# Adding the experts' rows to their tokens in memory instead of storing each pick and joining them at the end

## The chip, the cores and the metric
One NeuronCore of a Trainium2 chip runs the whole layer as one program. Five engines run instruction streams of their own and meet by semaphores: TensorE (PE), VectorE (DVE), ScalarE (ACT), GpSimd (POOL) and SyncE (SP). SP and POOL issue the transfers; sixteen DMA engines carry them. The metric is the device time of one execution in microseconds.

## The reference
A hybrid encoder layer over 768 tokens of width 1024 (512 "sample" tokens and 256 "prompt" tokens, each group with its own modulation vectors), all in f32: normalise, project, neighbourhood attention beside bidirectional RWKV-7, project, add; then a mixture of experts, add, and a final RMS norm. What matters here is the mixture and what follows it:

```
h   = rms_norm(x) * (1 + scale2) + shift2
pg  = softmax(h @ rg_w + rg_b)            # 4 groups, top 1
le  = (h @ re_w + re_b)[chosen group]     # 8 experts, top 2, weights renormalised
out[token] += w * ((silu(h @ w1[e]) * (h @ w3[e])) @ w2[e])      # two picks e per token, 32 experts
x   = x + gate2 * out
y   = rms_norm(x) * final_g
```

Expert weights are 32 x (w1, w3: 1024 x 512; w2: 512 x 1024), 201 MB in all.

## The kernel before
Tokens stand in six tiles of 128 (four of the sample group, two of the prompt group). The program has numbered phases; the change begins in phase 5.

**Phase 5, residual and routing.** For tile t = 1 to 5 (tile 0 is done earlier) TensorE multiplies by the output weights, VectorE adds the gated result to the input rows in `x2(t)` (`residual`, semaphore `x2_ready`, two halves a tile), normalises them to `h2` (`norm`, `h2_ready`), and SP stores `h2` to memory (`h2_rows`). TensorE transposes the rows (`turned`) and multiplies them by the router's weights (`routed`); VectorE makes the logits (`scores`). After the last tile VectorE alone selects the group and the two experts for all six tiles at once (`first_max`, three times, and masks `both_e`), TensorE counts ranks inside each expert by triangular products, VectorE turns a rank into a slot, and TensorE makes tables by one-hot products: `idx_all`, for every expert and each of its 64 slots the token to gather, and `put_all`, for the 128 half rows of its output the place to write. Experts with more than 64 tokens get further blocks from an overflow list in memory. `list_ready` is given at the end of VectorE's routing, when the list and the two weights of each token, `wts`, are there. Unused slots get an index outside the table and are skipped by the transfer.

**SP's queue in phase 5** is an order written by hand. Weights are kept in three slots of w1, w3 and w2. Slot 0 and w2 of slot 1 are loaded early. After `o5_mm` reaches 12 (the last product with the output weights) follow w1 of slot 1, the last tile's h2 store, w3 of slot 1 and w1 of slot 2, then w3 of slot 2, and behind `list_ready` the overflow lists and w2 of slot 2, the ninth load.

**Phase 6, experts.** Per expert e: GpSimd gathers 64 rows of h2 by an indirect DMA (`xg`, L2346); TensorE transposes them (L2442), multiplies by w1 and w3 (L2455, 64 products each 256 wide), ScalarE applies silu, VectorE multiplies (L2421), TensorE transposes (L2464), multiplies by w2 (L2473); VectorE copies the output from PSUM to `yb` (L2425: partition p < 64 is the first half of the row of slot p, partition 64 + p its second half); GpSimd scatters the 128 half rows of 2 KB to `y_dram`, which has a row for each of the two picks of each token (L2335). GpSimd's order is gather e, wait for the landing of scatter e - 4 (`freed`), scatter e - 3. As soon as TensorE has used a weight slot, SP loads the weights of expert e + 3 into it (L2309). The overflow blocks would follow in a loop at run time; in this data there are none. When TensorE has done all but the last two experts SP also loads the rows of gate2 (`g2_row`) and of final_g (`f_row`).

**Phase 7, join and final norm.** SP waits for `picks_out` and loads for each tile both picks (1 MB). For tile 0 ScalarE and VectorE weight and add them; for tiles 1 to 5 TensorE adds them by products with diagonal matrices of the weights (L2577), VectorE multiplies by the gate (L2546) and adds x2 (L2548). ScalarE squares with a running sum (L2528) and takes the root (L2529), VectorE takes the reciprocal (L2558) and scales (L2560), SP stores the tile (L2511).

Of the kernel before, what the change touches and what calls it, by code (L numbers as in the profile page):

```python
# [21 lines left out]
f16 = mybir.dt.float16  # L22
# [130 lines left out]
def build(nc, A, O, upto=4):  # L153
    ctx = ExitStack()
    with ctx:
# [32 lines left out]
        y_dram = dram("pick_out", [2 * TOK * 2, D // 2])  # L188
# [1663 lines left out]
        g2_row = take(2 * D).rearrange("p (g d) -> p g d", g=2)  # L1852
# [25 lines left out]
        idx_all = take(NBLK).bitcast(i32)  # L1878
# [5 lines left out]
        put_all = take(NBLK).bitcast(i32)  # L1884
# [43 lines left out]
        tmp_e = arena[:, top6:top6 + N2 * NE].rearrange("p (n e) -> p n e", e=NE)  # L1928
        wrap = take(NBLK)
        lsel = take(NT * NE).rearrange("p (t e) -> p t e", e=NE)  # L1930
        hits16 = take(NT * NE // 2).bitcast(f16).rearrange("p (t e) -> p t e", e=NE)
        rank12, first12, excl12, pos12, low12, base12 = (take(N2) for _ in range(6))
        level = take(N2 * (TOK // BLK - 1)).rearrange("p (n m) -> p n m", n=N2)
        rank16 = take(N2 * BLK // 2).bitcast(f16).rearrange("p (n s) -> p n s", n=N2)
        block16 = take(N2 * NBLK // 2).bitcast(f16).rearrange("p (n b) -> p n b", n=N2)
# [4 lines left out]
        o32 = take(NE)  # L1940
        assert top[0] <= at_prep, top[0]

        WEIGHTS = (("h1_mm", w1_f, w1_v), ("h3_mm", w3_f, w3_v), ("y_mm6", w2_f, w2_v))

        def sp_phase5(sp):
# [38 lines left out]
            sp.dma_start(slot_dram.rearrange("(b s) o -> b (s o)", s=BLK), over_idx[NE:NBLK]).then_inc(sem("list_out"), 16)  # L1984
            sp.dma_start(put_dram.rearrange("(b s) o -> b (s o)", s=2 * BLK), over_put[NE:NBLK]).then_inc(sem("list_out"), 16)
# [7 lines left out]
        def act_phase5(act, own):  # L1993
            for t in range(1, NT):
                if t == 3:
                    rec_out(act, NT - 2)
                    rec_out(act, NT - 1)
                h2T_evac(act, t - 1, 0)
                h2T_evac(act, t - 1, 1)
                tile_square(act, own, t, 0)  # L2000
                if t == NT - 1:
                    h2T_evac(act, t, 0)
                tile_square(act, own, t, 1)
            h2T_evac(act, NT - 1, 1)
            act.wait_ge(sem("g_centred"), 1)
            nc.scalar.activation(tg, tg, ACT.Exp).then_inc(sem("g_exp"), 1)
            act.wait_ge(sem("m_diff"), 1)
            nc.scalar.activation(m2, m2, ACT.Exp).then_inc(sem("m_exp"), 1)
# [44 lines left out]
        def dve_phase5(dve, own):  # L2053
# [9 lines left out]

            for t in range(1, NT):
# [11 lines left out]
            scores(NT - 1)  # L2076

            dve.wait_ge(sem("logit_ready"), NT)

            def b(ap, shape):  # L2080
                return ap.unsqueeze(len(ap.shape)).to_broadcast(shape)

            def first_max(one_hot, top_v, values, tmp, width):

                shape = [P, NT, width]
                own.link(nc.vector.tensor_reduce(top_v, values, AX, ALU.max))
                own.link(nc.vector.tensor_tensor(tmp, values, b(top_v, shape), ALU.is_equal))
                own.link(nc.vector.tensor_tensor(tmp, tmp, fall_row[:, 0:width].unsqueeze(1).to_broadcast(shape), ALU.mult))
                own.link(nc.vector.tensor_reduce(pk, tmp, AX, ALU.max))
                own.link(nc.vector.tensor_tensor(one_hot, tmp, b(pk, shape), ALU.is_equal))  # L2090

            pg = logit[:, :, 0:NG]
            first_max(og, gm, pg, tg, NG)

            le = logit[:, :, NG:].rearrange("p t (g e) -> p t g e", g=NG)
            own.link(nc.vector.tensor_tensor(lsel.rearrange("p t (g e) -> p t g e", g=NG), le, b(og, [P, NT, NG, EPG]), ALU.mult))
            own.link(nc.vector.tensor_reduce(s8, lsel.rearrange("p t (g e) -> p t e g", g=NG), AX, ALU.add))
            first_max(o1, m1, s8, t8, EPG)
            own.link(nc.vector.scalar_tensor_tensor(s8, o1, -1e30, s8, ALU.mult, ALU.add))
            first_max(o2, m2, s8, t8, EPG)  # L2100
            for one, o8 in ((both_e[:, 0], o1), (both_e[:, 1], o2)):
                own.link(nc.vector.tensor_tensor(one.rearrange("p t (g e) -> p t g e", g=NG), b(og, [P, NT, NG, EPG]),
                                                 o8.unsqueeze(2).to_broadcast([P, NT, NG, EPG]), ALU.mult))
            nc.vector.tensor_tensor(hits16, both_e[:, 0], both_e[:, 1], ALU.add).then_inc(sem("hits_ready"), 1)

            picks = both_e.rearrange("p k t e -> p (k t) e")
            pairs = [P, N2, NE]

            def picked(out, values):

                own.link(nc.vector.tensor_tensor(tmp_e.rearrange("p (k t) e -> p k t e", k=2), both_e, values, ALU.mult))
                own.link(nc.vector.tensor_reduce(out, tmp_e, AX, ALU.add))

            picked(first12, first_row.unsqueeze(1).unsqueeze(1).to_broadcast([P, 2, NT, NE]))
            dve.wait_ge(sem("rank_mm"), 2)
            own.link(nc.vector.tensor_copy(cnt_col[0:NE], bank[3][0:NE, 0:1]))
# [3 lines left out]
            picked(rank12, bank[2][:, 0:NT * NE].rearrange("p (t e) -> p t e", e=NE).unsqueeze(1).to_broadcast([P, 2, NT, NE]))  # L2120
            own.link(nc.vector.tensor_tensor(level, rank12.unsqueeze(2).to_broadcast([P, N2, TOK // BLK - 1]),
                                             first_row[:, 1:TOK // BLK].unsqueeze(1).to_broadcast([P, N2, TOK // BLK - 1]), ALU.is_ge))
            own.link(nc.vector.tensor_reduce(low12, level, AX, ALU.add))
            own.link(nc.vector.scalar_tensor_tensor(low12, low12, -float(BLK), rank12, ALU.mult, ALU.add))
            own.link(nc.vector.tensor_tensor(rank16, low12.unsqueeze(2).to_broadcast([P, N2, BLK]),
                                             rank_row.unsqueeze(1).to_broadcast([P, N2, BLK]), ALU.is_equal))
            nc.vector.tensor_tensor(rank16, rank16, token_row.unsqueeze(2).to_broadcast([P, N2, BLK]), ALU.mult).then_inc(sem("rank16_ready"), 1)
# [3 lines left out]
            picked(excl12, excl.unsqueeze(1).unsqueeze(1).to_broadcast([P, 2, NT, NE]))  # L2131
            own.link(nc.vector.tensor_scalar(base12, excl12, float(NE - 1), float(BLK), ALU.add, ALU.mult))
            own.link(nc.vector.tensor_tensor(base12, base12, first12, ALU.subtract))
            own.link(nc.vector.scalar_tensor_tensor(base12, rank12, float(BLK), base12, ALU.is_ge, ALU.mult))
            own.link(nc.vector.tensor_tensor(pos12, rank12, first12, ALU.add))
            own.link(nc.vector.tensor_tensor(pos12, pos12, base12, ALU.add))
            own.link(nc.vector.tensor_tensor(base12, pos12, low12, ALU.subtract))
            nc.vector.tensor_tensor(block16, base12.unsqueeze(2).to_broadcast([P, N2, NBLK]),
                                    block_row.unsqueeze(1).to_broadcast([P, N2, NBLK]), ALU.is_equal).then_inc(sem("block16_ready"), 1)
            dve.wait_ge(sem("idx_mm"), 1)  # L2140
            own.link(nc.vector.tensor_scalar(wrap[0:BLK], bank[5][0:BLK, 0:NBLK], float(-TOK), float(-TOK), ALU.is_ge, ALU.mult))
            nc.vector.scalar_tensor_tensor(idx_all[0:BLK], bank[5][0:BLK, 0:NBLK], float(2 * TOK), wrap[0:BLK], ALU.add, ALU.add).then_inc(sem("idx_ready"), 1)
            dve.wait_ge(sem("idx_mm"), 2)
            nc.vector.tensor_scalar(put_all, bank[2][:, 0:NBLK], 2.0, half_place, ALU.mult, ALU.add).then_inc(sem("put_ready"), 1)
# [7 lines left out]
            dve.wait_ge(sem("idx_mm"), 3)  # L2152
            own.link(nc.vector.tensor_scalar(tmp_e.rearrange("p n e -> p (n e)")[0:NBLK, 0:BLK], bank[3][0:NBLK, 0:BLK], float(-TOK), float(-TOK), ALU.is_ge, ALU.mult))
            nc.vector.scalar_tensor_tensor(over_idx[0:NBLK], bank[3][0:NBLK, 0:BLK], float(2 * TOK), tmp_e.rearrange("p n e -> p (n e)")[0:NBLK, 0:BLK], ALU.add, ALU.add)
            for j in range(2):
                nc.vector.tensor_scalar(over_put[0:NBLK, j * BLK:(j + 1) * BLK], bank[3][0:NBLK, 0:BLK], 2.0, float(4 * TOK + j), ALU.mult, ALU.add)
# [510 lines left out]
```

## Time and profile before

| | |
|---|---|
| median of three runs | 1367.01 us (1366.73 to 1368.69) |
| the profiled execution's own time | 1364.02 us |
| its span, first to last instruction | 1362.3 us |
| TensorE busy | 1162.7 us, 85% |
| VectorE busy | 416.6 us, 31% |
| ScalarE busy | 347.9 us, 26% |
| GpSimd busy | 280.0 us, 21% |
| moved by DMA | 314.74 MB, 231 GB/s over the span |
| granted TensorE clock, mean | 0.955 |

The page is one execution seen by the hardware profiler. Busy shares are means over stages that have different limits, so a stage is read by its windows and its waits. A line of the timeline has its start in microseconds from the span's beginning, its length, engine, source line and operation; in brackets stands how long the engine was idle before and who released it. An engine letter with q (SPq, POOLq) is that engine's queue at the moment of issue; the transfer itself then takes until its landing. The share of DMA can pass 1 by a few hundredths.

### The profile page before, as it was taken

Reading aid. Unit: us, or ns where it says so; the run is one execution under the profiler, and the core shown is the slowest. Engines: PE = TensorE matmul, PEld = TensorE weight load, DVE = VectorE, ACT = ScalarE, POOL = GpSimd, SP = SyncE. Lnnn points to the kernel's source line nnn. Section 1 sums busy time; section 2 is a strip of 40 time slices with the busy share of each in tenths; the row PEclk is TensorE's granted clock in tenths of the full one; section 3 lists DMA queues with packets and bytes.
Section 4 is the critical chain, followed back from the end, with each engine's and each line's share of the span. In section 5 each row is a group of like instructions: output and inputs, shape, how many; then the busy total and the mean of one; then the engine's idle time right before and its main releaser. Section 6 shows DMA issues by size and latency. Waiting matters only on the chain.

```text
span 1362.3 us, 29631 instructions
## 1 busy us (share of the span) xinstructions
PE 1162.7 (85%) x13063; PEld 721.1 (53%) x13063; DVE 416.6 (31%) x726; ACT 347.9 (26%) x749; POOL 280.0 (21%) x254
## 2 busy tenths in 40 slices
PE   4899999999996889988799939998877778778855
PEld 3465555564455778878655525554444444444432
DVE  2100044435655555665446360000000000000017
ACT  3210024443332555566422111010010010100002
POOL 0100002312245434367331001111111111111000
PEclk8999999999997999999999969998899998998897
DMA  9895141223254221230408079999999999999975
GB/s 316 290 338 207 31 139 63 78 85 107 95 172 114 50 50 28 50 81 4 179 32 324 31 283 381 390 394 405 401 396 406 400 404 404 396 396 402 414 284 223
DMA packets 82025, 314.74 MB, mean 231 GB/s; under 512 B 13808, under 2 KB 28488, under 8 KB 65150
## 3 DMA queue, kind: packets, MB, share of 16 engines
q1 hardware_dynamic: 75862, 298.96, 59.2%
q0 software_dynamic: 5120, 12.59, 2.6%
q8 instruction: 87, 1.43, 0.4%
q10 hardware_dynamic: 936, 1.61, 0.3%
q14 instruction: 20, 0.16, 0.0%
HBM read 291.58 MB, written 25.74 MB: 233 GB/s over the span
## 4 chain that ended last, share of the span: by engine, by line
PE 28%; DMA 27%; DVE 5%; ACT 4%; issue 2%; SPq 1%; POOL 0%; DVEq 0%; POOLq 0%; ACTq 0%
DMA arena<-in_exp_w 26%; PE bank L1568 10%; PE bank L2455 6%; PE bank L1838 6%; PE bank L2473 2%; PE bank L1592 2%; SPq L2309 1%; DVE arena L1449 1%; PE bank L2194 1%; DMA arena<-pick_out 1%; PE bank L2442 1%; DVE arena L1436 1%; ACT arena L1278 1%; DVE arena L2560 0%; PE bank L2577 0%
## 5 line engine op out<-in xcount | busy, mean ns | idle before, releaser
L2455 PE MATMUL bank<-arena 128*64 128x256 f32 x2048 | 253.6, 405 | 72.6 <-DMA arena<-in_exp_w 59.8
L888 PE MATMUL bank<-arena 128*128 128x512 f32 (+1 forms) x736 | 256.2, 496 | 4.1 <-DVE arena L488 2.0
L2455 PEld LDWEIGHTS bank<-arena 128*64 128x64 f32 x2048 | 157.9, 146 | 178.3 <-DMA arena<-in_exp_w 69.5
L1568 PE MATMUL bank<-arena 64*64 64x64 f16 (+3 forms) x7184 | 199.2, 217 | 37.0 <-issue 13.2
L1568 PEld LDWEIGHTS bank<-arena 64*64 64x64 f32 (+2 forms) x7184 | 177.3, 124 | 64.1 <-issue 36.5
L888 PEld LDWEIGHTS bank<-arena 128*128 128x128 f32 x736 | 133.8, 189 | 100.3 <-issue 86.1
L2473 PE MATMUL bank<-arena 128*64 128x512 f32 x512 | 116.9, 598 | 16.6 <-ACT arena L2399 16.6
L2421 DVE TENSOR_TENSOR arena<-bank,arena 128x256 f32<-128x256 f32 x32 | 13.6, 425 | 305.6 <-PE bank L2455 305.6
L2346 POOL DMA_INDIRECT arena<-h_scratch,arena x32 | 30.7, 960 | 363.3 <-PE bank L2442 267.2
L1838 PE MATMUL bank<-arena 128*128 128x512 f32 x192 | 86.4, 597 | 0.0
L2473 PEld LDWEIGHTS bank<-arena 128*64 128x64 f32 x512 | 34.0, 136 | 77.4 <-issue 54.7
L2425 DVE COPY arena<-bank 128x512 f32<-128x512 f32 x32 | 22.1, 692 | 164.4 <-PE bank L2473 164.4
L2386 ACT COPY arena<-bank 128x512 f32<-128x512 f32 x32 | 18.8, 586 | 202.6 <-PE bank L2442 202.6
L2335 POOL DMA_INDIRECT pick_out<-arena x32 | 32.4, 1011 | 172.8 <-DVE arena L2425 172.8
L2393 ACT ACTIVATE arena<-bank 128x256 f32<-128x256 f32 x32 | 12.3, 384 | 209.9 <-PE bank L2455 209.9
L448 POOL TENSOR_TENSOR arena<-arena 128x512 f32<-128x512 f32 x16 | 18.6, 1163 | 191.0 <-DVE arena L761 191.0
L1838 PEld LDWEIGHTS bank<-arena 128*128 128x128 f32 x192 | 34.9, 189 | 37.9 <-issue 37.3
L1462 DVE CAST arena<-bank 128x512 f16<-128x512 f32 x48 | 32.9, 686 | 38.9 <-PE bank L1568 38.9
L923 PE MATMUL bank<-arena 128*128 128x512 f32 x96 | 42.9, 598 | 0.0
L2442 PEld LDWEIGHTS bank<-arena 64*128 64x128 f32 x256 | 30.6, 199 | 16.3 <-issue 16.3
L722 DVE COPY arena<-bank 128x512 f32<-128x512 f32 (+1 forms) x8 | 4.5, 559 | 113.8 <-PE bank L888 113.7
L2442 PE MATMUL bank<-arena 64*128 64x64 f32 x256 | 35.0, 278 | 4.3 <-DMA arena<-h_scratch,arena 4.3
(262 smaller groups left out, 1276.5 us busy)
## 6 DMA issues: line engine op xcount, KB each, us to landing
arena<-in_exp_w SPq DMA_DIRECT2D x96, 2048.0 KB, 44.8
arena<-in_ada_w SPq DMA_DIRECT2D x12, 2048.0 KB
arena<-in_w_in SPq DMA_DIRECT2D x11, 1024.0 KB, 6.6
direction_scratch<-arena SPq DMA_DIRECT2D x6, 1536.0 KB, 6.1
arena<-direction_scratch SPq DMA_DIRECT2D x24, 384.0 KB, 5.6
arena<-pick_out SPq DMA_DIRECT2D x6, 1024.0 KB, 10.3
arena<-in_x_sample SPq DMA_DIRECT2D x8, 512.0 KB, 5.0
arena<-in_w_out SPq DMA_DIRECT2D x8, 512.0 KB, 7.1
```

What stands on the lines that cost most here:

```text
L888: return nc.tensor.matmul(bank[i % 3][:, 0:GR[p] * GW], w[:, k, :], hT[:, k, PART[p]], start=(k == 0), stop=(k == KD - 1))
L923: ins = nc.tensor.matmul(bank[i % 3], hT[:, k, c * P:(c + 1) * P], wv[:, k, :], start=(k == 0), stop=(k == KD - 1))
L1462: nc.vector.tensor_copy(nm[1 + l % 2][:, 1], bank[6].rearrange("p (j r c) -> p j r c", j=NPAIR, r=2)).then_inc(sem("nm_dve"), 1)
L1568: return nc.tensor.matmul(out, lhsT, r, start=start, stop=True, skip_group_check=True)
L1592: ins = nc.tensor.transpose(bank[q % 2][:, j * P:(j + 1) * P], src[:, j * P:(j + 1) * P], ident)
L1838: ins = nc.tensor.matmul(out_bank(t, hf), catT[:, k, t * P:(t + 1) * P], wout[k][:, hf * 512:hf * 512 + 512], start=(k == 0), stop=(k == K ...
L2335: nc.gpsimd.indirect_dma_start(y_dram, bass.IndirectOffsetOnAxis(ap=put_all.bitcast(u32)[:, e:e + 1], axis=0), yb[e % 2], None, bounds_che ...
L2346: nc.gpsimd.indirect_dma_start(xg[e % 2][0:BLK, :], None, h2_dram, bass.IndirectOffsetOnAxis(ap=idx_all.bitcast(u32)[0:BLK, e:e + 1], axis=0),
L2425: nc.vector.tensor_copy(yb[c.s], bank[6 + c.s]).then_inc(c.sem("y_ready6"), 1)
L2442: ins = nc.tensor.transpose(bank[0][:, j * BLK:(j + 1) * BLK], xg[c.s][0:BLK, j::KD], ident[0:BLK, 0:BLK])
L2455: ins = nc.tensor.matmul(bank[b + 2 * c.s][BLK * n:BLK * n + BLK, 0:HALF], xT[c.s][:, j, :], slot[c.w][:, j, n * HALF:(n + 1) * HALF], sta ...
L2473: ins = nc.tensor.matmul(bank[6 + c.s][BLK * n:BLK * n + BLK, :], hidT[:, j % 2, j // 2, :], w2_s[c.w][:, j, n * 512:(n + 1) * 512], start ...
```

## The change
Each expert's output is weighted while it is evicted from PSUM, and the scatter adds it to a table of token sums in memory.

- `y_dram` becomes `token_sum`, two half rows per token plus 256 spare half rows. In phase 5 SP stores `x2(t)`, the residual, there before it stores h2.
- The scatter has `compute_op=ALU.add`. Half rows of unused slots are no longer skipped but go to the spare half rows.
- Per expert two VectorE instructions make `gw`, the gate row of each slot's group times the slot's weight (for both groups; one of the two weights is zero), and the eviction is a product with `gw` instead of a copy. The gate rows (`g2_half`, four loads of 64 partitions x 2 KB) come in phase 5 and not near the end of phase 6. VectorE's loop over the experts is written out for all 32.
- A table of the slots' weights, `w_slot`, is made in phase 5 by 24 f32 products, and one for the overflow blocks by 12 more. TensorE waits for `w_slot_ready` before the experts. Two more small stores write the overflow's weights; they stand behind `list_ready`.
- Routing is split: `select` and `ranked` run for tiles 0 to 3 while tiles 4 and 5 are worked on and then for tiles 4 and 5. The main table now holds only the 32 main blocks, and its indices and places come from one product; overflow is treated after them.
- Phase 7 loads one tile of sums of 512 KB each and does only the final norm. TensorE has no work in it. `f_row` has a new place.

```diff
-        y_dram = dram("pick_out", [2 * TOK * 2, D // 2])
+        y_dram = dram("token_sum", [2 * TOK + 2 * P, D // 2])
+        wo_dram = dram("slot_weight", [2 * MAX_OVER * BLK, 1])
...
             def h2_rows(t):
+                sp.wait_ge(sem("x2_ready"), 2 * t + 2)
+                sp.dma_start(token_rows(t), x2(t)).then_inc(sem("sum_in"), 16)
                 sp.wait_ge(sem("h2_ready"), t + 1)
...
             weights(1, 2)
+            for g in range(2):
+                for h in range(2):
+                    at = 5 * D + h * (D // 2)
+                    sp.dma_start(g2_half[h * BLK:(h + 1) * BLK, g, :], mod_dram[g, at:at + D // 2].partition_broadcast(BLK)).then_inc(sem("g2_in"), 16)
             sp.wait_ge(sem("list_ready"), 1)
...
+            for g in range(2):
+                sp.dma_start(wo_dram[g * MAX_OVER * BLK:(g + 1) * MAX_OVER * BLK, :].rearrange("(b s) o -> b (s o)", s=BLK), sums_over[:, g, :]).then_inc(sem("list_out"), 16)
             weights(2, 2)
...
+            act.wait_ge(sem("rank16_ready"), 2)
+            nc.scalar.copy(rank32, rank16).then_inc(sem("rank32_ready"), 1)
+            act.wait_ge(sem("w_slot_mm"), 1)
+            nc.scalar.copy(w_slot, bank[6][:, 0:2 * NE].rearrange("p (g e) -> p g e", g=2)).then_inc(sem("w_slot_ready"), 1)
...
             for t in range(1, NT):
                 residual(dve, own, t)
                 scores(t - 1)
+                if t == NT_S:
+                    select(EARLY)
                 if t < NT - 1:
                     norm(dve, own, t)
+                if t == NT_S:
+                    ranked(EARLY, 1)
...
+            select(LATE)
+            own.link(nc.vector.tensor_tensor(m2, m2, m1, ALU.subtract))
+            nc.vector.tensor_tensor(tg, pg, b(gm, [P, NT, NG]), ALU.subtract).then_inc(sem("g_centred"), 1)
+            ranked(LATE, 2)
...
+            table(LATE).then_inc(sem("idx_mm"), 1)
+            pe.wait_ge(sem("rank32_ready"), 1)
+            pe.wait_ge(sem("w_pick_ready"), 1)
+            for g in range(2):
+                some = group_of_pick(g)
+                for i in some:
+                    for j in range(2):
+                        ins = nc.tensor.matmul(bank[6][j * BLK:(j + 1) * BLK, g * NE:(g + 1) * NE], rank32[:, i, :], w_pick[:, i, :],
+                                               start=(i == some[0]), stop=(i == some[-1]))
+            ins.then_inc(sem("w_slot_mm"), 1)
...
-            for g in range(2):
-                sp.dma_start(g2_row[:, g, :], mod_dram[g, 5 * D:6 * D].partition_broadcast(P)).then_inc(sem("g2_in"), 16)
...
                 if e == 0:
                     pool.wait_ge(sem("put_ready"), 1)
+                    pool.wait_ge(sem("sum_in"), 16 * NT)
...
-                                             bounds_check=4 * TOK - 1, oob_is_err=False).then_inc(sem(f"y_out{e % 2}"), 16)
+                                             bounds_check=2 * TOK + 2 * P - 1, oob_is_err=True, compute_op=ALU.add).then_inc(sem(f"y_out{e % 2}"), 16)
...
+                nc.vector.tensor_scalar(gw, g2_half[:, 1, :], share[1], None, ALU.mult).then_inc(c.sem("gw_done"), 1)
+                dve.wait_ge(c.sem("gw_done"), 2 * c.n + 1)
+                nc.vector.scalar_tensor_tensor(gw, g2_half[:, 0, :], share[0], gw, ALU.mult, ALU.add).then_inc(c.sem("gw_done"), 1)
...
-                nc.vector.tensor_copy(yb[c.s], bank[6 + c.s]).then_inc(c.sem("y_ready6"), 1)
+                dve.wait_ge(c.sem("gw_done"), 2 * c.n + 2)
+                nc.vector.tensor_tensor(yb[c.s], bank[6 + c.s], gw, ALU.mult).then_inc(c.sem("y_ready6"), 1)
+                dve.wait_ge(c.sem("y_ready6"), k)
...
+            pe.wait_ge(sem("w_slot_ready"), 1)
             rows(Main(0, 0, 0, 0, 0, 0))
...
             for t in range(NT):
-                sp.dma_start(ya[t], picks[t]).then_inc(sem(f"rows_in{t}"), 16)
+                sp.dma_start(x2(t), token_rows(t)).then_inc(back_in(t)[0], 16)
...
             for t in range(NT):
-                act.wait_ge(sem("joined"), t + 1)
+                act.wait_ge(*back_in(t))
```

The routing functions that are new (`select` has 21 instructions, those of before on the tiles `ts`):

```python
            def select(ts):
                n = ts.stop - ts.start
                dve.wait_ge(sem("logit_ready"), ts.stop)
                first_max(og, gm, pg, tg, NG, ts)
...
                nc.vector.tensor_tensor(hits16[:, ts], both_e[:, 0, ts], both_e[:, 1, ts], ALU.add).then_inc(sem("hits_ready"), 1)

            def table(ts):
                turn = 1 if ts is EARLY else 2
                pe.wait_ge(sem("rank16_ready"), turn)
                pe.wait_ge(sem("picks16_ready"), turn)
                for k in range(2):
                    for t in range(ts.start, ts.stop):
                        i = k * NT + t
                        for j in range(2):
                            ins = nc.tensor.matmul(bank[0][j * BLK:(j + 1) * BLK, 0:NE], rank16[:, i, :], picks16[:, i, :],
                                                   start=(i == 0), stop=(i == 2 * NT - 1))
                return ins
```

## Rows read from the trace of the kernel before

**Rows 1.** The page, 40 slices: busy share of the DMA engines in tenths.
```profile
DMA  9895141223254221230408079999999999999975
```

**Rows 2.** Windows: length, busy PE, PEld, DVE, ACT, POOL, clock, DMA share, GB/s.
```profile
1000.00:1200.00 200.00, 154.55 (x1086) 86.14 (x1088) 13.39 (x24) 17.68 (x39) 24.56 (x25) 0.97 1.01 402
...
1275.00:1291.00 16.00, 12.36 (x68) 6.47 (x68) 0.90 (x2) 1.24 (x3) 0.00 (x0) 0.79 1.01 425
```

**Rows 3.** Waits of 920 to 1300 us: engine, line, awaited, total us, times, longest.
```profile
PE bank L2455 <- DMA arena<-in_exp_w: 58.6, 25, 3.4
```

**Rows 4.** Timeline of SP's queue, 700 to 900 us: start, length, what, how many.
```profile
786.78 0.33 SPq L1948 DMA_DIRECT2D arena<-in_exp_w  x1
...
812.61 0.32 SPq L1983 DMA_DIRECT2D overflow_list<-arena  x1
...
813.98 0.41 SPq L1948 DMA_DIRECT2D arena<-in_exp_w  x1
```

**Rows 5.** The chain that ended last, 1270 us to the end: start, length, what.
```profile
1264.94 43.55 DMA arena<-in_exp_w
...
1319.10 2.54 DMA pick_out<-arena
```

**Rows 6.** DMA issues from 600 us: size and median us from issue to landing.
```profile
arena<-in_x_sample SPq DMA_DIRECT2D x4, 512.0 KB, 4.4
```

**Rows 7.** Timeline of the last stage, ScalarE and VectorE.
```profile
1333.55 1.28 ACT L2529 ACT_TABLE_LOAD   x1
...
1353.79 1.06 ACT L2528 ACTIVATE arena<-arena 128x1024 f32<-128x1024 f32 x1 [2.38 <-DVE arena L2548]
...
1354.76 0.19 ACT L2528 ACTIVATION_READ_ACCUMULATOR arena<-arena 128x1 f32 x1
...
1354.97 0.29 ACT L2529 ACTIVATE arena<-arena 128x1 f32<-128x1 f32 x1
...
1355.30 0.16 DVE L2558 RECIPROCAL arena<-arena 128x1 f32<-128x1 f32 x1
...
1355.50 1.28 DVE arena L2560
```

**Rows 8.** DMA queues in 1000 to 1200 us: packets, MB, share of 16 engines.
```profile
q1 hardware_dynamic: 6773, 76.17, 95.0%
...
q0 software_dynamic: 1920, 4.24, 6.0%
```

**Rows 9.** Windows of 2 us around the scatter issued at 971.68 us.
```profile
970.00:972.00 2.00, 2.00 (x22) 1.35 (x20) 0.69 (x1) 0.00 (x0) 0.32 (x1) 1.00 1.04 342
...
972.00:974.00 2.00, 1.60 (x16) 0.78 (x12) 0.00 (x0) 0.36 (x1) 0.69 (x1) 1.00 0.97 289
```

**Rows 10.** Windows of 20 us before the stream.
```profile
740.00:760.00 20.00, 20.00 (x69) 10.52 (x68) 6.02 (x9) 3.65 (x10) 0.00 (x0) 1.00 0.33 120
...
760.00:780.00 20.00, 20.00 (x71) 10.62 (x70) 7.08 (x10) 5.09 (x13) 0.00 (x0) 1.00 0.07 27
```

**Rows 11.** Windows around the ninth weight load.
```profile
810.00:815.00 5.00, 1.11 (x8) 0.95 (x8) 1.86 (x12) 1.02 (x3) 1.09 (x2) 0.50 0.37 96
...
817.00:818.00 1.00, 1.00 (x8) 0.62 (x6) 0.00 (x0) 0.00 (x0) 0.00 (x0) 0.50 0.96 295
```

**Rows 12.** Timeline of VectorE in the routing: first, second, and the indices.
```profile
791.26 0.18 DVE L2086 TENSOR_REDUCE arena<-arena 128x6 f32<-128x24 f32 x1
...
791.47 0.18 DVE L2087 TENSOR_TENSOR arena<-arena 128x24 f32<-128x24 f32 x1
...
807.72 0.21 DVE L2142 SCALAR_TENSOR_TENSOR arena<-bank,arena 64x56 int32<-64x56 f32 x1
```

**Rows 13.** Timeline of TensorE: the first expert's transposes.
```profile
813.26 1.11 PE L2442 MATMUL bank<-arena 64*128 64x64 f32 x8 [4.28 <-DMA arena<-h_scratch,arena]
```

**Rows 14.** The page's groups: busy us, mean ns, idle before, releaser.
```profile
L2421 DVE TENSOR_TENSOR arena<-bank,arena 128x256 f32<-128x256 f32 x32 | 13.6, 425 | 305.6 <-PE bank L2455 305.6
```

**Rows 15.** The tile of the scatters' target: all its DMAs, issue to landing.
```profile
DMA to landing us min/median/max: 2.5/8.3/15.3
```

More of the change, by code:

```diff
@@ L1883, in build @@
         over_put = take(2 * BLK).bitcast(i32)
[L1884 removed]
+        put_all = take(NE).bitcast(i32)
         put_o = take(1).bitcast(i32)
@@ L1940, in build, with back_in, token_rows, group_of_pick @@
         o32 = take(NE)
+        put_a, put_b = take(NE), take(NE)
         assert top[0] <= at_prep, top[0]
+        EARLY, LATE = slice(0, NT_S), slice(NT_S, NT)
         WEIGHTS = (("h1_mm", w1_f, w1_v), ("h3_mm", w3_f, w3_v), ("y_mm6", w2_f, w2_v))
+        def back_in(t):
+            return (sem(f"x5_in{t}"), 16 * (NT_P if t == NT_S else 1) + 16) if t <= NT_S else (sem("last_back"), 16)
+        def token_rows(t):
+            return y_dram[2 * t * P:2 * (t + 1) * P, :].rearrange("(p h) n -> p (h n)", h=2)
+        def group_of_pick(g):
+            return [k * NT + t for k in range(2) for t in range(NT) if group(t) == g]
         def sp_phase5(sp):
@@ L2100, in dve_phase5 @@
[L2100 to L2116, printed above, removed]
+            select(LATE)
@@ L2173, in turned @@
                 for hf in range(2):
+                    if hf and between:
+                        between()
                     pe.wait_ge(sem("x2_ready"), 2 * j + hf + 1)
@@ L2202, in pe_phase5 @@
                 if t == NT - 1:
+                    ranks(EARLY)
                     turned(t - 1)
@@ L2213, in pe_phase5 @@
                     rec_turned(pe, NT - 2)
-            turned(NT - 1)
+            turned(NT - 1, between=lambda: table(EARLY))
             routed(NT - 1)
-            pe.wait_ge(sem("x2_ready"), 2 * NT)
-            pe.wait_ge(sem("hits_ready"), 1)
-            hits = hits16.rearrange("p t e -> p (t e)")
-            n = NT * NE
-            nc.tensor.matmul(bank[2][:, 0:n], before16, hits, start=True, stop=False)
-            for s in range(1, NT):
-                ins = nc.tensor.matmul(bank[2][:, s * NE:n], ones16, hits[:, 0:n - s * NE], start=False, stop=(s == NT - 1))
@@ L2224, in pe_phase5 @@
-            ins.then_inc(sem("rank_mm"), 1)
-            for t in range(NT):
-                ins = nc.tensor.matmul(bank[3][0:NE, 0:1], hits16[:, t, :], ones16[:, 0:1], start=(t == 0), stop=(t == NT - 1))
-            ins.then_inc(sem("rank_mm"), 1)
+            ranks(LATE)
+            for t in range(NT):
+                ins = nc.tensor.matmul(bank[7][0:NE, 0:1], hits16[:, t, :], ones16[:, 0:1], start=(t == 0), stop=(t == NT - 1))
+            ins.then_inc(sem("rank_mm"), 1)
+            table(LATE).then_inc(sem("idx_mm"), 1)
@@ L2483, in pe_phase6 @@
             overflow(pe, over, overflow_count(pe))
-        top[0] = P + 2
-        ya = [take(2 * D).rearrange("p (k d) -> p k d", k=2) for _ in range(NT)]
         top[0] = ARENA - WEXP
```

287 lines of the change are left out of this document (152 added, 135 removed).

## The prediction

> **What bounds the kernel now.** I read the page's forty slices first: the DMA engines are idle or half used for most of the first half and then stand at nine tenths or more from slice 25 to slice 38 [rows 1]. In 1000 to 1200 us their share is 1.01 at 402 GB/s, while TensorE is busy for only 154.55 of 200 us [rows 2]. Next I read the waits of 920 to 1300 us: TensorE waited 25 times for expert weights [rows 3]. So the expert stage is a stream of 96 loads of 2 MB on SP's queue, nearly all of it behind 786.78 us, when the load after the last projection is issued [rows 4]; what makes that stream longer is added to the end in full, and what TensorE, VectorE or GpSimd do beside it is free as long as it stays inside a period of about 16.5 us. Last I read the chain that ended last: the weights issued at 1264.94 land at 1308.5, the last expert is finished, its scatter lands at 1321.64, and from there the last stage runs alone to 1362.3 [rows 5]. The change touches three things: the opening of the stream (routing), its content (the scatters), and the last stage. I price each.
>
> **The last stage (saves).** Before, 40.7 us lie between the last landing and the end of the span [rows 5]. After, no picks are loaded, no product by the diagonal is made (40 matmuls), and no gate, sum or join is left on VectorE; a tile of sums of 512 KB is loaded where the residual stood, ScalarE squares it, VectorE scales it. Hop from landing to SP's issue 0.4 and the issue 0.4; a 512 KB load lands in 4.4, as the x loads did [rows 6]; ScalarE loads its table once, 1.28, and does six tiles at 1.06 + 0.18 + 0.29 = 1.53 us with gaps [rows 7], so 9.2; the six loads are all in within 8 us and VectorE needs 1.28 + 0.17 per tile, so ScalarE sets the pace. Then the last scale, 1.5, and the last store, 5.5 (from 1356.8 to 1362.3 [rows 7]). Sum 0.8 + 4.4 + 1.3 + 9.2 + 1.5 + 5.5 = 22.7, a saving of 18.0. The last scatter now reads before it writes; it took 2.54 [rows 5] and I give it 1.2 more (0.5 to 3). Net **-17**.
>
> **The scatters (cost).** In 1000 to 1200 us the load queue moved 76.17 MB [rows 8]. Where no scatter or gather is issued the engines move 425 GB/s [rows 2]; those bytes alone would take 179.2 us, so 20.8 us went to the 12.1 experts' pairs of a gather and a scatter (76.17 MB by 6.29 MB an expert), 1.72 us a pair. A gather and a scatter move 1536 picks x 4 KB / 32 = 197 KB each, 0.46 us at 425. The gather I take at that, so a scatter costs 1.26 us, more than twice its bytes. The two slices around one scatter say the same: 342 and 289 GB/s in place of 425 for 2 us each [rows 9], 1.03 us lost and 0.46 of its own, 1.5. After, two things change. Unused slots are no longer skipped but sent to 256 spare half rows: 128 rows of 2 KB and not 96, so 1.7 us. And each row is added: its old content must be read too. Nothing in this trace shows an adding DMA, so I bound it. From below: the added bytes written, 65 KB or 0.15 us, and the read hidden beside the write; less than nothing is excluded, since every byte that moved before still moves. From above: adding doubles the whole scatter, 3.4 us, +2.1. In between, the read is charged like the gather's, 262 KB at 425 GB/s, 0.62 us: 2.3 us in all, **+1.0** a scatter, my value, as the gather is the nearest row of a read from memory by rows. 31 scatters, issued from 832.05 to 1304.54, lie before the last weights land: **+31**; bounds +5 and +65.
>
> The trace shows that plain scatters already cost more than their bytes [rows 8, 9]; it does not show why. The Trainium skill ("Collectives: The Full Stack", section "The bandwidth ceiling: the fold count and why AG ≠ RS ≠ AR") says that an add in the DMA datapath is slow not for the arithmetic but because it needs two source reads, both on one ring, and that reduce-scatter ran at about half the rate of a copy. No trace here shows it; by that rule the scatter would double, which is the upper bound and the second rival.
>
> **The opening of the stream (cost).** The first three loads go out at 717, the engines are a third busy in 740 to 760 and 0.07 in 760 to 780 [rows 10], and four more follow from 786.78. The ninth waits for the overflow list at 812.6 and goes out at 813.98 [rows 4]; the queue had run dry, 0.37 busy in 810 to 815, and full rate is back at about 817.2 [rows 11]. After:
> - Routing of the first four tiles is done ahead, in VectorE's gaps of tile 4 and 5. TensorE has no gap there: five or so products of 0.06 us, +0.3 to 0.4 on all that follows.
> - For the last two tiles the 21 selecting instructions shrink little, since at 24 elements they are already 0.18 long in steps of 0.21 [rows 12]: 4.3 us and not 5.7. Two subtractions, the ranks (0.3), eight ranking instructions (2.3), the table on TensorE and two more (1.3): indices ready at about 800.3, before 807.9 [rows 12]. Gathers go out 7.6 us earlier.
> - But TensorE may not start the experts: it stands behind the weight table, 24 small products at 0.14 each by the eight 64 x 64 ones that took 1.11 at half clock [rows 13], done at 806.6; then the overflow's product, nine VectorE instructions (3.5), and 12 + 12 products (0.6 and 2.4 plus latency): 813.5, before 813.26 [rows 13]. The gain of 7.6 is gone.
> - The list is ready after eight more VectorE instructions, 815.4 (+2.9), and two more small DMAs of 0.45 each stand before the ninth load: issued 817.8, **+4**, and nothing else in the stream makes up for it, as what follows was already back to back. New traffic in front of it, the last residual tile (512 KB) and four gate loads of 128 KB, 1.05 MB or 2.5 us, fills part of the hole and is not added again. Bounds -1 and +7: the hole of 5 us is all that could be won.
>
> **Costed at nothing.** Stores of five residual tiles, 1.3 us each of engine time, lie in the idle stretch 745 to 786 or before weights that are not needed until 815; SP waits on x2_ready first, which always precedes the h2_ready that it waits on anyway. Two VectorE instructions per expert for the gate (about 1.4 us) and the wait for its own write: VectorE idled 305.6 us before the hidden product [rows 14]; they run while TensorE does the next w1, which takes 3.4. If that cover went, 32 x 1.4. Eviction times gate is as long as the copy. GpSimd waits for the residual stores before scatter 0, 40 us after they landed; behind it stand freed and the gathers, not late. The gate rows of 2 x 512 KB loaded at 1290 go, but they stood behind the last weights. The unrolled VectorE loop issues what it did.
>
> **Sum.** The profiled execution took 1364.0 (span 1362.3 and 1.7 around). 1364.0 + 4 + 31 - 17 = 1382. The median of the runs shown, 1367.0, is 3.0 above the profiled one: **1385.0**.
>
> **Rivals.**
> - *The add rides along* (faster). The engines read the old row while they stream the new one, and only the bytes written count: +5 for +31, 1359. It decides from below 0.3 us a scatter. For: read and write are two sides of a DMA, and the share of the software queue is small [rows 8]. Against: the stream already pays 1.26 us for 0.46 us of bytes.
> - *Only the spare rows cost*: +0.4 x 31 = 13, 1367, no change.
> - *Adding doubles the scatter*: +65, 1419. [...]
> - *The landing chain binds.* Scatter e goes out only when e - 1 has landed. Landings took 8.3 at the median, 15.3 at most, in periods of 16.5 [rows 15]; if adding doubled the median, 16.6 + 1.0 of issue, each period grows by about 1 and yb comes free late; beyond that it grows one for one, 1420 and more.
>
> **Chances.** Forecast 0.38 (its own range 1370 to 1400), rides along 0.22, spare rows only 0.10, doubled 0.22, landing chain 0.08. Two executions differ by some 0.2% (about 2.7 us), so faster means under 1364.3: rides along and part of the next, 0.26; same 0.09; slower 0.65. Range 1358 to 1422, from the first rival to just past the doubled one.
>
> **What would show it.** The load queue's bytes in 1000 to 1200 us: 76.17 MB in periods of 16.5 us before; 75 MB or more would be the first rival, 72 my forecast (17.5 us), 68 the doubled one (18.6 us). First expert transposes at 813.5 and the ninth load at 817.8. From the last landing to the end 22 us, not 40.7. If TensorE's waits are no longer for weights but for gathers or for yb, the sum is wrong in kind.

## The result, and the profile after

The change made the kernel slightly slower: 1370.06 us median (1365.70 to 1374.48, 18 runs) against 1367.01 (18 runs of the kernel before beside them), a ratio of 1.0027 with the interval 1.0015 to 1.0039, or +3.7 us. A second series (x6 below) gave 1.0038 (1.0024 to 1.0052), +5.2 us; I use the mean of both, +4.4. The forecast was +18. The direction was right, the size off by 14 us. The profiled execution has a span of 1365.1 us.

Below, a ratio is turned into microseconds by 1367, so +4.4 stands for a mean ratio of 1.0032. Single profiled executions differ by up to 5 us in when the stream begins (783.97 to 788.99 us), so effects are taken from ratios, and traces serve for where they sit and as a check.

The slices of the page after, to be held against [rows 1]: the hole in slice 24 is filled, nothing else stands out.

```profile
DMA  9895141232254222130427199999999999999995
```

Windows (columns as in [rows 2]), of the opening and of the stream. From 805 to 820 us the engines were never short of work, where before they were at 0.37 in 810 to 815 [rows 11]. The stream moves 392 GB/s where it moved 402 [rows 2].

```profile
805.00:810.00 5.00, 3.63 (x39) 3.45 (x40) 2.46 (x11) 0.00 (x0) 0.00 (x0) 0.50 1.01 310
810.00:815.00 5.00, 4.13 (x26) 2.58 (x26) 1.31 (x8) 0.58 (x1) 0.93 (x1) 0.53 1.00 287
815.00:820.00 5.00, 5.00 (x50) 3.18 (x46) 1.24 (x2) 1.67 (x2) 0.00 (x0) 1.00 1.03 325
...
1000.00:1200.00 200.00, 158.66 (x1042) 89.78 (x1040) 26.34 (x45) 15.81 (x36) 32.95 (x23) 0.93 1.02 392
```

The DMA queues in 1000 to 1200 us, which answer to [rows 8]: the load queue moved 2.88 MB less, and the packets of GpSimd's queue took 11.3% of the sixteen engines' time, not 6.0%.

```profile
q1 hardware_dynamic: 6500, 73.29, 90.7%
q0 software_dynamic: 2590, 5.04, 11.3%
```

SP's queue in the opening, which answers to [rows 4]. The first load after the projections is at 784.25 and the ninth at 813.47, 29.2 us later; before it was 27.2.

```profile
784.25 0.33 SPq L1972 DMA_DIRECT2D arena<-in_exp_w  x1
...
788.92 7.24 SPq L1972 DMA_DIRECT2D arena<-in_exp_w  x3
796.20 2.39 SPq L2011 DMA_DIRECT2D arena<-mod_scratch  x4
811.47 0.33 SPq L2013 DMA_DIRECT2D overflow_list<-arena  x1
...
813.47 0.41 SPq L1972 DMA_DIRECT2D arena<-in_exp_w  x1
```

TensorE's timeline between the routing and the first expert: the 24 products of the weight table (which leave 48 records), the overflow's products, the transposes of [rows 13] and the first weights.

```profile
799.76 2.78 PE L2328 MATMUL bank<-arena 128*64 128x32 f32 x48 [3.20 <-DVE arena L2195]
...
806.99 2.75 PE L2339 MATMUL bank<-arena 128*24 128x64 f32 x24
809.67 1.14 PE L2557 MATMUL bank<-arena 64*128 64x64 f32 x8
811.68 3.61 PE L2570 MATMUL bank<-arena 128*64 128x256 f32 x18 [0.87 <-ACT arena L2487]
```

The chain that ended last, as in [rows 5]. It still runs through a weight load. The last scatter takes 4.76 us (2.54 before), lands at 1344.74, and 20.4 us remain to the end of the span; before they were 40.7.

```profile
1328.33 0.04 issue
1328.38 3.70 PE bank L2570 x32
...
1339.98 4.76 DMA token_sum<-arena
...
1345.15 3.28 DMA arena<-token_sum
1348.45 1.15 ACT arena L2629 x2
1349.62 1.28 ACT L2630
...
1359.28 1.28 DVE arena L2638
```

TensorE's waits of 920 to 1300 us, as in [rows 3]: still for weights. GpSimd has a new wait, for the landing of a scatter, ahead of its gather; no wait of TensorE for a gather follows from it.

```profile
PE bank L2570 <- DMA arena<-in_exp_w: 46.1, 27, 3.0
...
POOL arena L2447 <- DMA token_sum<-arena: 60.6, 6, 10.3
```

So three sizes are in question: what a stored scatter costs, what the add costs on top, and what the opening cost. The experiments take these one by one.

### The profile page after: what moved, and what is told of

Same layout as the page of the kernel before. It is cut to its first block, busy times and chain, and to the rows that moved or that the text cites. A ratio compares the mean times of both kernels' runs of the same rounds, so it can differ in the third digit from the quotient of the medians.

```text
span 1365.1 us, 29717 instructions
## 1 busy us (share of the span) xinstructions
PE 1162.9 (85%) x13087; PEld 729.0 (53%) x13087; DVE 444.7 (33%) x800; ACT 347.3 (25%) x750; POOL 309.1 (23%) x254
## 4 chain that ended last, share of the span: by engine, by line
DMA 29%; PE 28%; ACT 5%; DVE 4%; issue 2%; SPq 1%; POOL 0%; DVEq 0%; ACTq 0%; POOLq 0%
DMA arena<-in_exp_w 28%; PE bank L1569 10%; PE bank L2570 6%; PE bank L1839 6%; PE bank L2588 2%; PE bank L1593 2%; SPq L2408 1%; DVE arena L1450 1%; PE bank L2293 1%; PE bank L2557 1%; DVE arena L1437 1%; ACT arena L2629 1%; ACT arena L1279 1%; ACT arena L1269 0%; DVE arena L1467 0%
## 5 line engine op out<-in xcount | busy, mean ns | idle before, releaser
L2570 PE MATMUL bank<-arena 128*64 128x256 f32 x2048 | 262.9, 415 | 76.0 <-DMA arena<-in_exp_w 53.2
L2570 PEld LDWEIGHTS bank<-arena 128*64 128x64 f32 x2048 | 164.2, 149 | 186.6 <-issue 66.9
L2436 POOL DMA_INDIRECT token_sum<-arena x32 | 60.9, 1904 | 181.5 <-DVE arena L2538 167.7
L2533 DVE TENSOR_TENSOR arena<-bank,arena 128x256 f32<-128x256 f32 x32 | 13.6, 424 | 270.6 <-PE bank L2570 270.6
L2588 PEld LDWEIGHTS bank<-arena 128*64 128x64 f32 x512 | 37.6, 138 | 83.7 <-issue 55.1
L2538 DVE TENSOR_TENSOR arena<-bank,arena 128x512 f32<-128x512 f32 x32 | 22.1, 691 | 173.9 <-PE bank L2588 173.9
L2494 ACT ACTIVATE arena<-bank 128x256 f32<-128x256 f32 x32 | 12.3, 383 | 249.4 <-PE bank L2570 249.4
L1314 ACT CAST arena<-bank 128x512 f16<-128x512 f32 x60 | 35.6, 593 | 4.5 <-PE bank L1569 4.4
```

The costliest lines, as they stand in the source:

```text
L1314: nc.scalar.copy(xs[3 if l == XP else 1 + l % 2].rearrange("p g j c -> p (g j c)"), bank[7]).then_inc(sem("x_ready"), 1)
L2436: nc.gpsimd.indirect_dma_start(y_dram, bass.IndirectOffsetOnAxis(ap=put_all.bitcast(u32)[:, e:e + 1], axis=0), yb[e % 2], None, bounds_che ...
L2570: ins = nc.tensor.matmul(bank[b + 2 * c.s][BLK * n:BLK * n + BLK, 0:HALF], xT[c.s][:, j, :], slot[c.w][:, j, n * HALF:(n + 1) * HALF], sta ...
L2588: ins = nc.tensor.matmul(bank[6 + c.s][BLK * n:BLK * n + BLK, :], hidT[:, j % 2, j // 2, :], w2_s[c.w][:, j, n * 512:(n + 1) * 512], start ...
```

## The experiments

Every kernel was timed beside the kernel before: x2, x6, x9 and x10 twelve times, the others, whose output is not the layer's, four to six times. "After" is the changed kernel; a minus sign means faster than before.

**Stored or added, 128 or 96 half rows (x1, x2, x3).** The three differ from the kernel after only in the arguments of the scatter:

```diff
-    bounds_check=2 * TOK + 2 * P - 1, oob_is_err=True, compute_op=ALU.add)
+    bounds_check=2 * TOK + 2 * P - 1, oob_is_err=True)                     # x1: stores, 128
+    bounds_check=2 * TOK - 1, oob_is_err=False, compute_op=ALU.add)        # x2: adds, spare rows skipped
+    bounds_check=2 * TOK - 1, oob_is_err=False)                            # x3: stores, spare rows skipped
```

In x1 and x3 the sums are not formed: a store overwrites what stood there. x2 computes everything.

> The changed kernel with its scatter storing instead of adding; all 128 half rows still go out. It leaves out the summing, so the output is not the layer's. Theory A, a price per half row that the add raises a little (from the traces: 1.26 us for 96 stored, 1.96 us for 128 added, so 13 and 15 ns a half row): 31 x 0.28 = 9 us less than the changed kernel, about 1361. Theory B, the spare half rows are free and the whole +0.70 us per expert is the add: 31 x 0.70 = 22 less, 1348. Theory C, the stream pays the time for which a lone scatter holds the sixteen engines (2.08 us added against 0.51 x 128/96 = 0.68 stored): 43 less, 1327. Last stage as in the changed kernel (20 us) in all three.

> The changed kernel with the index bound set so that half rows of unused slots are skipped, as the kernel before did; the add stays and the result is the same. Theory A: 32/128 of 1.96 us less per scatter, 0.49 x 31 = 15 less than the changed kernel, about 1355, faster than both kernels. Theory B (spare rows free): no change, 1370. Theory C: a quarter of 2.08, 0.52 x 31 = 16 less, 1354; it differs from A in the other runs. A lone last scatter holds the engines for about 1.6 us and not 2.08 by C and by A alike.

> The changed kernel with both undone: the scatter stores and skips unused slots, just the traffic of the kernel before; it leaves out the summing. Theories A and B: 0.70 x 31 = 22 less than the changed kernel, about 1348, and a period of 16.7 us per expert as before. Theory C: 49 less, 1322. If it is much above 1348, something other than the scatters (the gate rows' VectorE work, the opening) lengthens the stream.

| kernel | half rows | mode | ratio (interval) | us against before |
|---|---|---|---|---|
| after, two series | 128 | add | 1.0027 (1.0015 to 1.0039), 1.0038 (1.0024 to 1.0052) | +4.4 |
| x1 | 128 | store | 0.9892 (0.9870 to 0.9915) | -14.8 |
| x2, two series | 96 | add | 0.9971 (0.9959 to 0.9983), 0.9961 (0.9946 to 0.9976) | -4.6 |
| x3 | 96 | store | 0.9874 (0.9857 to 0.9891) | -17.2 |

The add costs 19.2 us (some 3.5 uncertain) on 128 half rows, 0.60 us a scatter over 32, and 12.6 (some 3 uncertain) on 96, 0.39 each. About 2 us of the 19.2 are the last scatter, which stands on the chain (4.76 us for 2.70 in x1); the other 31 cost some 0.55 each. Spare rows cost 2.4 us when stored, within the intervals of nothing, and 9.0 us (0.28 each) when added. Of the theories, C is out: it asked for 43 us between after and x1, and 19.2 were measured. A and B are both right on x3 (22 less, 21.6 measured) and each is wrong on a part: A gave the add 9 us, and B gave the spare rows of x2 nothing. The rate of the stream agrees: x3's load queue moved 76.44 MB in 1000 to 1200 us, no less than before.

```profile
q1 hardware_dynamic: 6786, 76.44, 95.1%
q0 software_dynamic: 1926, 4.24, 5.9%
```

**No rows scattered, then none gathered (x4, x7).** Each is the kernel after with an index bound of 0, so that all but index 0 is skipped by the transfer: in x4 the scatters write next to nothing of the experts' rows, in x7 the gathers also bring next to none, so the experts work on what lies in the buffer.

```diff
-    bounds_check=2 * TOK + 2 * P - 1, oob_is_err=True, compute_op=ALU.add)
+    bounds_check=0, oob_is_err=False, compute_op=ALU.add)                  # x4 and x7
-    bounds_check=TOK - 1, oob_is_err=False)
+    bounds_check=0, oob_is_err=False)                                      # x7, the gather
```

> The changed kernel with an index bound of 0, so that hardly any half row leaves; GpSimd still issues every scatter. It leaves out the experts' part of the sum. Gives the whole price of a scatter in the stream. Theory A: 1.96 x 31 = 61 less than the changed kernel, 1309. Theory B the same total. Theory C: 2.08 x 31 = 64 less, 1306. If the scatter's excess over its bytes came from the gather instead (0.46 + 0.80 both ways swapped), only 1.16 x 31 = 36 less, 1334.

> The changed kernel with neither scatters nor gathers (index bound 0 for both; the experts compute on what stands in their buffers). It leaves out the gather of the rows and the experts' part of the sum. x4_none showed that a stored scatter of 96 half rows costs only 0.43 us and not 1.26, so the excess over the bytes that I charged to scatters must lie elsewhere. Theory D, in the gather: 1.3 us each, so 40 us less than x4_none, about 1295, and over 84 MB of weights in 1000 to 1200 us. Theory E, in neither, 425 GB/s just isn't the rate of a long stream: the gather costs its bytes, 0.46, 14 less, 1321, and 78 to 79 MB.

x4 ran at 0.9776 (0.9759 to 0.9792), -30.6 us; x7 at 0.9430 (0.9408 to 0.9453), -77.9 us. So the 32 stored scatters of x3 cost 13.4 us together (some 3 us uncertain), **0.42 each**, what their 197 KB take at 425 GB/s (0.46), and not the 1.26 of the prediction. The 32 gathers cost 47.3 us (some 4 uncertain), **1.48 each** for as many bytes, three times what I gave them. The pair was priced about right (1.90 measured, 1.72 predicted) and charged to the wrong half. Of the expectations for x4 the swapped one (36 us less than after) met the 35.0 measured, and for x7 theory D (40 less than x4, 47.3 measured) came near. The gathers were switched off only where no rows were scattered; how the two act together is not measured.

A check from the profiled executions, one of each (x5, x6 and x10, which is x2 again, are told below): the time from the first load after the projections to the landing of the last scatter. For x4 and x7 it is read from these lines:

```profile
785.80 0.33 SPq L1972 DMA_DIRECT2D arena<-in_exp_w  x1
...
1308.17 2.69 DMA token_sum<-arena
```

```profile
787.29 0.33 SPq L1972 DMA_DIRECT2D arena<-in_exp_w  x1
...
1262.88 2.69 DMA token_sum<-arena
```

| kernel | first load to last scatter's landing, us |
|---|---|
| before; x5 | 534.9; 535.8 |
| after; x6 | 560.5; 561.2 |
| x1 | 539.7 |
| x2; x10 | 552.8; 549.7 |
| x3 | 536.1 |
| x4 | 525.1 |
| x7 | 478.3 |

By this measure 32 gathers cost 46.8 us, 32 stored scatters 11.0, the add 21.2 on 128 half rows and 15.1 on 96: the same picture within 3 us. The load queue's bytes in 1000 to 1200 us order the kernels in the same way but are too coarse for the smallest price: 76.44 MB in x3 and 77.11 in x4 would be 0.14 us a scatter.

The queues of x4, then of x7, in 1000 to 1200 us:

```profile
q1 hardware_dynamic: 6877, 77.11, 97.0%
q0 software_dynamic: 2768, 2.36, 4.2%
```

```profile
q1 hardware_dynamic: 7555, 84.66, 100.4%
q0 software_dynamic: 3056, 0.02, 0.9%
```

They show where a gather's time goes. Without gathers a megabyte of weights occupies the engines for 200.8 / 84.66 = 2.37 us, with gathers for 194.0 / 77.11 = 2.52. In 77.11 MB that is 11.1 us, 0.91 for each of the 12.3 gathers in the window. The gathers' own packets take 3.3% of 200 us (4.2 less 0.9 for skipped indices), 0.54 each. 0.91 + 0.54 = 1.45: most of a gather's price is that the weights' packets beside it become slower. Why they do is not shown.

And the dips of 2 us that I had read as the scatter's [rows 9] are the gather's. In x4, where no rows are scattered, they stand as deep; in x7 they are gone:

```profile
1000.00:1002.00 2.00, 2.00 (x22) 1.34 (x20) 1.80 (x3) 0.00 (x0) 0.90 (x1) 1.00 1.02 342
1002.00:1004.00 2.00, 1.54 (x16) 0.71 (x10) 0.14 (x1) 0.38 (x1) 0.78 (x1) 1.00 0.97 285
```

```profile
1000.00:1002.00 2.00, 1.84 (x18) 1.26 (x20) 0.00 (x0) 0.00 (x0) 0.00 (x0) 1.00 1.04 422
1002.00:1004.00 2.00, 2.00 (x20) 1.18 (x17) 0.06 (x1) 0.00 (x0) 0.00 (x0) 1.00 1.09 447
```

**The last stage alone (x5).** The kernel before, whose last stage loads per tile 512 KB of the first picks' rows into `x2(t)` and does the final norm alone. Weights, gate, sum and residual are left out of its result.

```diff
-                sp.dma_start(ya[t], picks[t]).then_inc(sem(f"rows_in{t}"), 16)
+                sp.dma_start(x2(t), y_dram[2 * t * P:2 * (t + 1) * P, :].rearrange("(p h) n -> p (h n)", h=2)).then_inc(sem(f"rows_in{t}"), 16)
...
-                act.wait_ge(sem("joined"), t + 1)
+                act.wait_ge(sem(f"rows_in{t}"), 16)
...
-                join(t)
-            pe_phase7(pe)
```

> The kernel before with the last stage of the changed one: per tile one load of 512 KB (of the first pick's rows) into the residual's place and only the final norm; weighting, joining, gate and residual are left out of the output. Scatters, routing and stream are those of before. My theory: the last stage falls from 40.7 to 20.4 us, so 20 us less than the kernel before, about 1347 (ratio 0.985). Rival: the last scatter's landing and not the amount of work holds the stage (first load late, stores in line), then under 12 us less, 1355 or more.

0.9870 (0.9848 to 0.9892), -17.8 us (some 3 uncertain), where I had predicted 18.0. It also bears on the opening: x3 has the opening of the kernel after, scatters of as many rows as before's, and the short last stage; x5 has before's opening. x3 less x5 is +0.6 us, with some 4 us of uncertainty, where I had said +4. The ratios alone do not quite exclude +4; in the profiled executions above the two differ by 0.3 us and x3 from the kernel before by 1.3.

**The kernel after again (x6)**, unchanged, beside x5:

> The changed kernel unchanged, on the chip of this call, for the comparison. Both theories: ratio to the kernel before 1.0027 within 0.0015, last stage 20.4 us, period of the scatters 17.4 us, weights of the last expert awaited until 544 us after the load that follows the last projection.

1.0038 (1.0024 to 1.0052), median 1371.83. This is the second series of the table above.

**The gate loads of the opening (x8).** x3 without the four loads of gate rows and without the wait for them; the gate rows' values are left out.

```diff
-                    sp.dma_start(g2_half[h * BLK:(h + 1) * BLK, g, :], mod_dram[g, at:at + D // 2].partition_broadcast(BLK)).then_inc(sem("g2_in"), 16)
...
-            dve.wait_ge(sem("g2_in"), 16 * 4)
```

> As x3_plain_96 (the scatter stores and skips), and the four loads of the gate rows left out, so that VectorE multiplies by what stands in their place; it leaves out the gate and the summing. Tells why the opening did not cost 4 us. Theory F, the hole before the ninth load swallows new traffic and the ninth load's delay is what counts: no change against x3_plain_96 (1348), within 1.5 us. Theory G, the ninth load's delay is hidden and the gate loads (2 KB from one row to 64 partitions) hold the queue: 3 us less, 1345.

0.9857 (0.9835 to 0.9880), -19.5 us, 2.3 less than x3 with 3.9 of uncertainty. Whether the 524 KB cost their 1.2 us, more or nothing is not settled.

**Weighted at eviction, stored, joined by TensorE (x9).** The scatter stores each pick as before, x2 stays in SBUF, and the last stage loads 1 MB a tile and sums x2 and both picks by products with the identity.

```diff
+                for hf in range(2):
+                    nc.tensor.matmul(bank[2 * (t % 4) + hf], ident, x2(t)[:, hf * 512:hf * 512 + 512], start=True, stop=False)
...
+                    for k in range(2):
+                        ins = nc.tensor.matmul(bank[2 * (t % 4) + hf], ident, ya[t][:, k, hf * 512:hf * 512 + 512], start=False, stop=(k == 1))
```

> A version meant to be right and faster: rows weighted at eviction as in the changed kernel, but stored per pick (96 half rows, unused skipped) and never added in memory; the residual stays in SBUF, its stores go; the last stage loads both picks (1 MB a tile) and TensorE adds residual and both picks by products with the identity, ScalarE and VectorE read PSUM. Stream as x3_plain_96. Last stage paced by the loads, 2.6 us a tile instead of 1.5, and one tile of TensorE work: 29 us against 20.5. My theory: 1348 + 9 = 1357, ratio 0.993, 4 us below x2_add_96. Rival: TensorE at half clock after its idle time paces the stage, 5 us a tile: 1370.

1.0038 (1.0024 to 1.0052), +5.2 us: slower than before, and my expectation missed by 15. The stream ran like x3's (76.39 MB in the same 200 us); the loss is all in the last stage, 46.5 us from the last landing to the end where x3 has 20.8. TensorE's timeline of one tile there, and ScalarE's idle time before a tile:

```profile
1338.14 1.88 PE L2616 MATMUL bank<-arena 128*128 128x512 f32 x4
1339.86 3.60 PE L2621 MATMUL bank<-arena 128*128 128x512 f32 x8
```

```profile
1343.49 1.02 ACT L2641 ACTIVATE arena<-bank 128x1024 f32<-128x1024 f32 x1 [3.71 <-PE bank L2621]
```

A tile has six products and leaves twelve records. I had sized a product by one record, 0.43 us; it takes 0.86. So a tile takes TensorE 5.15 us and not 2.6, and ScalarE waits 3.71 us before each of the last four. The rival in the expectation named 1370, near the 1372.07 measured, but by luck: it rested on a half clock, and the granted clock was 0.50 only until 1330 us, in the first tile, and 0.99 to 1.00 from there on.

**The best version again (x10)**, x2's edit beside x9:

> x2_add_96 unchanged, on the chip of this call beside x9_store_and_join: ratio to the kernel before 0.997 as then. If x9 is faster than this one by the 4 us of its working, storing and joining in the last stage beats adding in memory; if it is slower, adding with the unused slots skipped is the better use of the change.

0.9961 (0.9946 to 0.9976), median 1361.90. Adding, but skipping unused slots, beats the kernel before by 0.3 to 0.4% in both series, and the kernel after by some 9 us.

## Why the prediction was right and wrong

**The bound was right.** A stream of weight loads sets the end. The times of the scatter variants stand in the order of the load queue's bytes in 1000 to 1200 us (73.29 MB after, 74.79 in x2, 75.56 in x1, 76.44 in x3, 77.11 in x4), and VectorE's two new instructions per expert (0.49 + 0.75 us), the longer eviction wait and GpSimd's longer issue stayed hidden.

**The last stage was right** within what can be told: 18.0 us predicted, 17.8 (some 3 uncertain) measured alone in x5. That the two agree to 0.2 is luck. From the last landing to the end the traces show 20.4 us and not 22.7, a saving of 20.3: the first load landed in 3.3 us for my 4.4, and 4.5 us lie behind the last scaling for my 5.5. The last scatter took 2.2 us more than before where I gave it 1.2.

**The step that failed is the sentence "The gather I take at that, so a scatter costs 1.26 us".** [rows 8] gives a loss of 1.72 us for a pair, and nothing in them says whose it is. I gave the gather its bytes and the scatter the rest; x4 and x7 show the reverse, 0.42 and 1.48. [rows 9] seemed to confirm the choice, but a gather issued 5 us before was still in flight there (a gather's landing takes 9 us), and x4 keeps the dip without scatters. A window is not evidence for one transfer when another is open in it. The error went into the sum through the spare rows: a third more of 1.26 is 0.42, or 13 us over 31 scatters; a third more of 0.42 is 0.14, and x1 less x3 gives 2.4 us in all. These 10.6 us are most of the 13.6 by which the forecast was off.

**The price of the add was right in size**: 0.62 predicted as the read of 262 KB at the stream's rate, 0.60 measured on 128 half rows (0.11 uncertain). That it is such a read is not shown: by the same working 96 half rows would cost 0.46, a doubling of the stored scatter would cost 0.49 and 0.42, and the measured 0.60 and 0.39 fit both within their uncertainty. The prices go by the rows: against x4, a stored scatter costs 0.42 (96 half rows) and 0.49 (128), an added one 0.81 and 1.09, so 4 us per thousand half rows stored and 8.5 added. A spare row, once added, costs as much as a used one, which is why the spare rows are 9.0 us and the best version leaves them out. Stored and added together I had charged them 18: 13, and 5 as their share of the read. All scatters together: predicted 31 + 1.2, measured 21.6 (after less x3), 10.6 us too much.

**By the rule of the Trainium skill** quoted before ("Collectives: The Full Stack", section "The bandwidth ceiling: the fold count and why AG ≠ RS ≠ AR"), two source reads should double the scatter. The runs agree within their uncertainty, from 0.49 to 1.09 and from 0.42 to 0.81. The rival built on it, that adding doubles the scatter, still missed the time (1419 for 1370), since it doubled 1.7 us for 128 half rows where 0.49 was measured.

**The opening cost about 1 us, not +4.** The ninth load was 2.0 us later against the first one, not 3.8, and TensorE reached the experts 25.4 us after the first load where I had 26.7 (before: 26.5). More important, I charged the ninth load's delay in full although 1.05 MB of new traffic stood ahead of it and kept the engines busy through the old hole; in 40 us from the first load, the load queue had moved 13.29 MB, 1.05 of them new, against 12.47: 0.23 MB of weights or 0.5 us behind. In the other profiled kernels with the new opening and gathers (x1 to x4, x6, x10) it was 12.96 to 13.25 MB, so up to 1.3 us. A late issue costs only what the engines then idle, plus the bytes that fill the hole.

**The sum again, with measured terms**: -17.8 for the last stage, +0.6 for the opening, +21.6 for the scatters, +4.4 in all. It closes because each term is a difference between two of the kernels; the check on the sizes is the table of profiled executions above. Against the forecast's 18.0 that is 10.6 off for the scatters, 3.4 for the opening and 0.2 for the last stage.

**The other rivals.** That the add rides along is refuted: it costs 12.6 to 19.2 us. That only the spare rows cost is refuted too, though its time, 1367, was by luck the nearest of all: the add is most of the cost. The landing chain did not bind: landings grew from 8.3 [rows 15] to 11.7 us at the median in periods of 17.4, and no wait of TensorE follows from the 60.6 us that GpSimd waited for them.

## What to carry to other kernels

Where two transfers share a loss, switch each off alone before pricing either; and a change to the one then costs in proportion to its own share. An accumulating scatter cost about twice a storing one here, unused rows included, so it should skip the rows that nobody reads. In a stage bound by a stream of loads, count bytes and idle time of the engines, not the lateness of an issue.

## What was not expected of the hardware

- A gather of 48 rows of 4 KB costs a stream of loads 1.48 us for 197 KB, and a scatter of as many bytes 0.42. Most of the difference is in the loads' packets, 2.52 against 2.37 us of engine time per MB. The cause is open.
- A lone added scatter of 128 half rows occupies the engines over three times as long as a lone stored one. GpSimd's queue in the 4 us around the last scatter of the kernel after, then around that of x1 (packets, MB, share of 16 engines):

```profile
q0 software_dynamic: 144, 0.26, 52.1%
```

```profile
q0 software_dynamic: 80, 0.26, 16.1%
```

That is 2.08 against 0.64 us, in 144 packets against 80, yet in the stream adding 128 half rows costs only 0.60 more. So the time that an added row's packets take alone is not what they take from the packets beside them. The last scatter, which stands on the chain, does pay it: 4.76 us for 2.70 in x1.
- GpSimd is busy (rows: count, busy us, mean ns, idle before and what ended it) for 1.90 us to issue an added scatter of 128 half rows, 1.38 for a stored one and 1.01 in the kernel before (with unused slots skipped):

```profile
L2436 POOL DMA_INDIRECT token_sum<-arena x32 | 60.9, 1904 | 181.5 <-DVE arena L2538 167.7 <-DMA token_sum<-arena 13.8
```

```profile
L2436 POOL DMA_INDIRECT token_sum<-arena x32 | 44.2, 1382 | 170.6 <-DVE arena L2538 170.6
```
- An f32 product of 128 x 512 with a 128 x 128 matrix leaves two records of 0.43 us, so 0.86 a product; the 40 records of the old join were 20 products. The products by w1 and w3 are counted by records too where the kernel before is described: its loops make 32 an expert, 256 wide, and the trace has 2048 records (L2455) for 32 experts, two for each.
